# Moving the load of the last norm's scales and shifts ahead of the gathered rows in the sync engine's queue

## The chip, the cores and the metric

One NeuronCore of a Trainium2 chip runs one program. The metric is the device time of one execution in microseconds, lower being better. The kernel before was timed three times: median 1456.06 us, lowest 1455.17, highest 1457.25.

## The reference, cut to what matters

The program computes one layer of a streaming encoder on 320 tokens of width 1024 (256 of a prompt, 64 of a running stream): an input norm, a projection, three token mixers, an output projection with a norm, and then a mixture of 64 experts with a last norm. Only that last part is touched here:

```
s     = sigmoid(t @ w_router); the 8 best experts of each token, from the 4 best of 8 groups
gates = the chosen s, divided by their sum, times 2.5
hid   = silu(t @ exp_w1[e]) * (t @ exp_w3[e])
moe   = sum over the chosen e of gates[e] * (hid @ exp_w2[e])  +  the shared expert
y     = layer_norm(2**0.25 * t + moe) * ln2_g + ln2_b
```

The two vectors `ln2_g` and `ln2_b`, 1024 floats each, are the last norm's scales and shifts. All of it is float32.

## The kernel before, in words

**Experts.** The 64 experts are worked off as 32 pairs (`NP`). For pair n the tensor engine (PE) gathers the pair's tokens (`gather`, L1250), multiplies them by the up weights (`hidden`, L1283, matmuls on L1290), turns the result (`turn`, L1294, on L1298) and multiplies it by the down weights (`down`, L1301, on L1309). VectorE (DVE) makes the product of the two halves of the hidden rows (`hid_step`, L2560). The 128 result rows of a pair are scaled and, for pairs 0 to 29, written by GpSimd with an indirect DMA into a DRAM table `expert_rows` that has eight slots for each token (`scatter`, L2840). The last two pairs are not written: PE adds them on chip with one-hot matrices (`combine`, L1315, on L1320).

**Weights.** SyncE (SP) issues all weight loads from one queue. Each expert has 2 MB of up weights (`up_weights`, L642) and 1 MB of down weights (`down_weights`, L645), in a ring of three pairs. The up weights of pair n are issued when the hidden matmuls of pair n-3 are done, and its down weights when all of pair n-3 is done (L663 to L669). So the last two issues, the down weights of pair 31, come when pair 28 is done.

**Gathered rows.** Then SP waits until pair 29 is done and its rows have been written (L679, L680) and loads the table back in five pieces of 2 MB, `ROWS[0]` to `ROWS[4]`. Pieces 1 to 4 are `rows_in(0)` to `rows_in(3)` (L671 to L684): two pieces for each of the first two groups of 128 tokens. The fourth waits for pair 30, too, since its place holds that pair's weights. Piece 5 (L689) holds the last 64 tokens.

**The change's own line.** Between piece 4 and piece 5, SP loads `ln2_g` and `ln2_b` into the tile `LN2` (L685 to L687): two loads of 512 KB, each one row of 4 KB that is read for all 128 partitions. Before them stands a wait for the gather of pair 24 (`x_done`), since `LN2` lies where the rows of that and of earlier pairs were fetched to (`XR`, L282).

**The sums.** DVE folds piece 1 once before it makes the hidden rows of the last pair (L2610 to L2612), then adds piece 1 to the shared expert's rows, piece 2 after it (`sum_rows`, L327, with L331, L333 and L336), and tells PE with `added`, count 1 (L2636). Then it folds piece 3 and adds the shared rows (count 2, L2639), and folds piece 4 once (count 3, L2640). PE waits for count 1 ahead of L1388 (`add_kept`, L1328), for count 2 ahead of the first part of L1395 and for count 3 ahead of its second part, which ends the sums of token group 1. Piece 5 goes to PE without DVE (L1398 to L1402).

**The norm.** For each group of tokens in turn DVE waits for `tokens` (L2672), and, from group 1 on, takes the mean and the variance itself (L2680 to L2686). It scales by `LN2` and writes `y` (L2690, L2696). ScalarE (ACT) does these sums for group 0, makes the reciprocal roots and copies half of `LN2` for the last group (L1795 to L1810). DVE waits for `LN2` on L2670, ACT on L1804. SP writes `y` out, group by group (L704 to L709).

Of the kernel before, what the change touches and what calls it, by code (L numbers as in the profile page):

```python
# [17 lines left out]
D = 1024  # L18
# [60 lines left out]
FETCHED = (3, 4, 5, 6, 7, 8, 12, 18, 24)  # L79
# [7 lines left out]
def hybrid_layer(nc, io):  # L87

    ctx = ExitStack()
    with ctx:  # L90
        sems = {}

        def sem(name):
            if name not in sems:
                sems[name] = ctx.enter_context(nc.semaphore(name))
            return sems[name]
# [34 lines left out]
        def shaped(v, *shape):  # L131
            names = "abcd"[:len(shape)]
            if len(shape) <= 1:
                return v
            return v.rearrange(f"p ({' '.join(names)}) -> p {' '.join(names)}",
                               **{k: s for k, s in zip(names[1:], shape[1:])})
# [143 lines left out]
        SHID, LN2 = shaped(CON[:, C_RST:C_RST + 2 * NTOK], 2, NTOK), shaped(HT[:, 0:2 * D], 2, D)  # L280
# [28 lines left out]
        def unit_in(u, i):  # L309

            ring, _, n = unit_weights(u)
            if ring is WOS:
                return f"early_in_or_rows_in{i}", n
            return f"weights_in{i}", 16 * ((NT + RING - 1 - i) // RING + 3 + n)
# [65 lines left out]
        def _(sp):  # L380
# [290 lines left out]
            def rows_in(k):  # L671
                t = k // 2
                if k < 4:
                    rows = slots[t * 1024:t * 1024 + 1024, :].rearrange("(p k) d -> p k d", k=8)[:, k % 2 * 4:k % 2 * 4 + 4, :]
                else:
                    rows = slots[2048 + (k - 4) * 256:2304 + (k - 4) * 256, :].rearrange("(p k) d -> p k d", k=4)
                sp.dma_start(ROWS[k][0:128 if k < 4 else 64], rows).then_inc(sem(f"early_in_or_rows_in{k}"), 16)

            sp.wait_ge(sem("pair_done"), SENT)  # L679
            sp.wait_ge(sem("rows_out"), SENT + 2)  # L680
            for k in range(4):
                if k == 3:
                    sp.wait_ge(sem("pair_done"), SENT + 1)
                rows_in(k)  # L684
            sp.wait_ge(sem("x_done"), FETCHED[-1] + 1)  # L685
            for k in range(2):
                sp.dma_start(LN2[:, k, :], io['lnv'][4 + k:5 + k, :].to_broadcast([128, D])).then_inc(sem("ln_in"), 16)  # L687
            rows = slots[2048:SLOTS, :].rearrange("(p k) d -> p k d", k=4)
            sp.dma_start(ROWS[4], rows).then_inc(sem("x_first_or_halves_in"), 16)  # L689
            with sp.If(more > 0):  # L690
# [2009 lines left out]
        def _(pool):  # L2700
# [106 lines left out]
            def token_sums(q):  # L2807

                B11, B12, B21, B22 = (OTS[q][:, k * KH:k * KH + KH, h] for k in range(2) for h in range(2))
                T1, T2, _, T4 = MSUM[q]  # L2810
                ptt(T1, B12, B11, sub)
                pool.drain()
                ptt(T2, B22, T1, sub)
                pool.drain()
                ptt(T4, B21, T2, sub)
                pool.drain()
# [205 lines left out]
```

## Time and profile before

| what | us |
|---|---|
| median of three runs | 1456.06 |
| lowest and highest run | 1455.17, 1457.25 |
| the profiled execution's own time | 1456.23 |
| its span, from the first to the last instruction | 1454.4 |
| PE busy in the span | 1424.0 |
| DVE busy in the span | 723.6 |

The rows below all belong to the profiled execution, and their times count from the start of its span. It took 0.17 us more than the median, and 1.8 us of it lie outside the span. A busy PE is modelled from the starts of pipelined matmuls, so a share near 100% says that it was always fed and not that it ran at its peak. A DMA is issued by an engine's queue and lands when the last of the 16 DMA engines has written its share.

### The profile page before, as it was taken

What the parts mean: (1) busy time and instruction counts of PE and PEld (TensorE: products, weight loads), DVE (VectorE), ACT (ScalarE), POOL (GpSimd) and SP (SyncE); (2) the same over time, 40 slices, a digit from 0 to 9 for tenths busy, and PEclk for the clock granted to TensorE, in tenths of its full rate; (3) what the DMA queues carried; (4) which work ended last, traced back from release to release, by engine and by line L of the source; (5) the groups of instructions that cost most, each with busy time, mean ns of one, the idle gap of its engine ahead of it and who ended that gap; (6) DMA issues with size and microseconds to landing.
All of it is one profiled execution on the core that took longest, in us unless ns stands there. A gap on an engine that the chain in (4) does not pass through costs nothing.

```text
span 1454.4 us, 32377 instructions
## 1 busy us (share of the span) xinstructions
PE 1424.0 (98%) x13553; PEld 1032.2 (71%) x13553; DVE 723.6 (50%) x1360; ACT 411.4 (28%) x847; POOL 220.6 (15%) x183
## 2 busy tenths in 40 slices
PE   7999999999999999999999999999999999999997
PEld 6999677677776777777778985864476766757752
DVE  7442778887655677735457664523312112111217
ACT  2333444443422454434532211111111111111112
POOL 3784113130110000020013000011010000100000
PEclk9999999999999999999999999999999999999999
DMA  8896473754244544566567639699999999999986
GB/s 282 192 192 156 127 218 107 202 173 135 73 130 141 141 116 120 184 185 188 158 227 206 214 119 387 238 407 410 427 425 428 428 428 428 427 427 428 428 353 281
DMA packets 157761, 375.74 MB, mean 258 GB/s; under 512 B 102224, under 2 KB 110816, under 8 KB 139824
## 3 DMA queue, kind: packets, MB, share of 16 engines
q1 hardware_dynamic: 141792, 346.64, 67.5%
q0 software_dynamic: 7152, 16.85, 3.4%
q10 hardware_dynamic: 8672, 10.20, 2.0%
q8 instruction: 105, 1.72, 0.5%
q14 instruction: 40, 0.33, 0.1%
HBM read 329.24 MB, written 51.95 MB: 262 GB/s over the span
## 4 chain that ended last, share of the span: by engine, by line
PE 83%; DMA 7%; DVE 5%; DVEq 1%; ACT 1%; issue 1%; SPq 0%; ACTq 0%
PE PS L723 22%; PE PS L1290 13%; PE PS L740 7%; PE PS L1309 6%; PE PS L1136 6%; DMA region<-moe_w 5%; PE PS L1257 5%; PE PS L807 3%; PE PS L1178 2%; DVE region L1815 2%; DVE region L1822 2%; PE PS L1117 2%; PE PS L1262 1%; PE PS L1200 1%; PE PS L815 1%
## 5 line engine op out<-in xcount | busy, mean ns | idle before, releaser
L723 PE MATMUL PS<-h0T,region 128*128 128x320 f32 x1360 | 390.3, 438 | 1.8 <-issue 1.6
L1422 ACT ACTIVATE region<-PS 128x320 f32<-128x320 f32 (+5 forms) x351 | 145.8, 427 | 669.5 <-PE PS L723 227.5
L723 PEld LDWEIGHTS PS<-h0T,region 128*128 128x128 f32 x1360 | 251.6, 190 | 109.7 <-issue 13.1
L1290 PE MATMUL PS<-region 128*64 128x512 f32 x1024 | 228.2, 592 | 3.0 <-DMA region<-moe_w 3.0
L1290 PEld LDWEIGHTS PS<-region 128*64 128x64 f32 x1024 | 118.1, 137 | 104.6 <-issue 53.1
L1815 DVE TENSOR_TENSOR region<-region 128x512 f32<-128x512 f32 (+10 forms) x237 | 164.7, 714 | 41.0 <-DMA region<-expert_rows 7.8
L1422 ACT ACTIVATE region<-region 128x256 f32<-128x256 f32 (+10 forms) x229 | 99.5, 465 | 109.6 <-DVEq L2235 24.5
L1309 PE MATMUL PS<-region,history 128*64 128x512 f32 x512 | 119.2, 597 | 1.4 <-ACTq L1755 0.5
L1815 DVE TENSOR_TENSOR history<-region,PS 128x256 f32<-128x256 f32 x32 | 13.5, 421 | 202.0 <-ACTq L1750 201.9
L1422 ACT ACT_TABLE_LOAD x77 | 98.8, 1283 | 24.9 <-ACTq L1469 9.5
L1822 DVE SCALAR_TENSOR_TENSOR region<-region,feature_vectors 128x320 f32<-128x320 f32 (+1 forms) x103 | 76.8, 746 | 56.3 <-ACTq L1498 41.1
L1257 PEld LDWEIGHTS PS<-region,h 128*128 128x128 f32 x736 | 85.8, 192 | 16.1 <-issue 15.9
L1257 PE MATMUL PS<-region,h 128*128 128x128 f32 x736 | 92.0, 278 | 0.0
L1309 PEld LDWEIGHTS PS<-region,history 128*64 128x64 f32 x512 | 52.6, 137 | 42.8 <-issue 21.3
L2540 DVE COPY region<-PS 128x512 f32<-128x512 f32 x32 | 22.1, 692 | 122.0 <-PE PS L1273 96.8
L1136 PE MATMUL PS<-region 128*128 128x160 f32 x528 | 74.1, 299 | 0.3 <-ACTq L1695 0.3
L1136 PEld LDWEIGHTS PS<-region 128*128 128x128 f32 x528 | 72.5, 190 | 0.6 <-issue 0.5
L1422 ACT ACTIVATE region<-PS,region 128x512 f32<-128x512 f32 (+1 forms) x35 | 24.5, 699 | 146.6 <-PE PS L1309 146.3
L740 PE MATMUL PS<-region 128*128 128x160 f32 x448 | 65.4, 299 | 0.0
L740 PEld LDWEIGHTS PS<-region 128*128 128x128 f32 x448 | 62.4, 190 | 0.0
L1815 DVE TENSOR_TENSOR region<-region,PS 128x160 f32<-128x160 f32 (+3 forms) x95 | 43.2, 489 | 34.7 <-PE PS L740 14.7
L807 PEld LDWEIGHTS PS<-region 64*64 64x64 f32 x2720 | 49.8, 134 | 14.3 <-issue 12.0
(248 smaller groups left out, 1579.8 us busy)
## 6 DMA issues: line engine op xcount, KB each, us to landing
region<-moe_w SPq DMA_DIRECT2D x65, 2048.0 KB, 29.1
region<-moe_w SPq DMA_DIRECT2D x65, 1024.0 KB, 27.5
region<-w_in SPq DMA_DIRECT2D x115, 512.0 KB, 5.9
region<-wo SPq DMA_DIRECT2D x32, 512.0 KB, 4.4
expert_rows<-region SPq DMA_DIRECT2D x20, 512.0 KB, 7.0
region<-expert_rows SPq DMA_DIRECT2D x5, 2048.0 KB, 18.7
projected<-region ACTq DMA_DIRECT2D x59, 167.5 KB, 3.9
region<-projected SPq DMA_DIRECT2D x10, 768.0 KB, 6.6
```

What stands on the lines that cost most here:

```text
L723: last = mm(PS[:, 6 + i % 2, 0:NTOK], WR[:, i, k, :], H0T[:, k, :], start=(k == 0), stop=(k == KT - 1))
L740: last = mm(out, lhs(k), rhs(k), start=start and k == 0, stop=k == KH - 1, skip_group_check=True)
L807: last = mm(head(out(j), 1 - x if across and j > 3 else x), head(lhs(j), x), head(rhs(j), x), **kw)
L1117: last = mm(PS[:, b, 0:NTOK], WR[:, q, k, :], OT[:, 8 * q + k, :], start=(k == 0 and q < 3), stop=(k == KT - 1 and q != 2))
L1136: last = mm(out, lhs(k), rhs(k), start=start and k == 0, stop=k == KH - 1, skip_group_check=True)
L1178: last = mm(PS[:, 2 * t + h, :], MG[:, k, t * 128:t * 128 + 128], WOUT[:, k, h * 512:h * 512 + 512], start=(k == 0), stop=(k == KT - 1))
L1257: last = mm(bank(h, 4, 128)[:, k], H0[:, t, (4 * h + k) * 128:(4 * h + k) * 128 + 128], OH[:, p, t, :], start=(h == 0 and k == 0 and t == ...
L1290: last = mm(PS[tiles(i), 2, :], XE[:, k, tiles(i)], W13[r][i][:, k * 512:k * 512 + 512], start=(k == 0), stop=(k == KT - 1))
L1309: last = mm(PS[tiles(i), 5 + h, :], HIDT[:, f, tiles(i)], W2[r][i][:, f * D + h * 512:f * D + h * 512 + 512], start=(f == 0), stop=(f == 1))
L1422: return nc.scalar.activation(out, in_, f, **kw)
L1815: return dve.tensor_tensor(out, a, b, op)
L1822: return dve.scalar_tensor_tensor(out=out, in0=a, scalar=s, in1=b, op0=op0, op1=op1)
```

## The change

The wait for `x_done` and the two loads of `LN2` move, unaltered, from between piece 4 and piece 5 to a place behind the down weights of the last pair and ahead of the waits for pair 29 and its written rows.

```
+            sp.wait_ge(sem("x_done"), FETCHED[-1] + 1)
+            for k in range(2):
+                sp.dma_start(LN2[:, k, :], io['lnv'][4 + k:5 + k, :].to_broadcast([128, D])).then_inc(sem("ln_in"), 16)
             sp.wait_ge(sem("pair_done"), SENT)
             sp.wait_ge(sem("rows_out"), SENT + 2)
             for k in range(4):
                 if k == 3:
                     sp.wait_ge(sem("pair_done"), SENT + 1)
                 rows_in(k)
-            sp.wait_ge(sem("x_done"), FETCHED[-1] + 1)
-            for k in range(2):
-                sp.dma_start(LN2[:, k, :], io['lnv'][4 + k:5 + k, :].to_broadcast([128, D])).then_inc(sem("ln_in"), 16)
             rows = slots[2048:SLOTS, :].rearrange("(p k) d -> p k d", k=4)
             sp.dma_start(ROWS[4], rows).then_inc(sem("x_first_or_halves_in"), 16)
```

## Rows read from the trace of the kernel before

**Rows 1.** Page, part 4: the chain that ended last, whole span, by engine.
```profile
PE 83%; DMA 7%; DVE 5%; DVEq 1%; ACT 1%; issue 1%; SPq 0%; ACTq 0%
```

**Rows 2.** Chain of waits, 1421 us to the end: start, length, what.
```profile
1421.95 3.63 PE PS L1320 x8
1425.58 0.23 PE PS L1298 x2
...
1426.30 3.65 PE PS L1309 x16
...
1432.75 1.72 PE PS L1328 x4
...
1437.19 5.36 PE PS L1395 x12
...
1442.57 0.70 DVE region L2680
```

**Rows 3.** Timeline of DVE from 1410 us: start, length, instructions [idle before <-releaser].
```profile
1420.65 2.29 DVE L1815 TENSOR_TENSOR region<-region 128x2048 f32<-128x2048 f32 x1 [7.78 <-DMA region<-expert_rows]
1423.03 0.42 DVE L1815 TENSOR_TENSOR history<-region,PS 128x256 f32<-128x256 f32 x1
...
1426.18 2.29 DVE L331 TENSOR_TENSOR region<-region 128x2048 f32<-128x2048 f32 x1
...
1429.85 1.23 DVE L336 TENSOR_TENSOR region<-region 128x1024 f32<-128x1024 f32 x1
1431.19 7.30 DVE L1815 TENSOR_TENSOR region<-region 128x2048 f32<-128x2048 f32 x4
1439.31 1.28 DVE L1822 SCALAR_TENSOR_TENSOR region<-PS,region,h0T 128x1024 f32<-128x1024 f32 x1 [0.81 <-ACTq L1793]
```

**Rows 4.** Timeline of PE and its weight loads, 1437 us to 1447 us.
```profile
1438.58 0.19 PEld L1395 LDWEIGHTS PS<-region,constants 128*128 128x128 f32 x1 [0.31 <-DVEq L2590]
...
1442.37 1.02 PE L1326 MATMUL PS<-region,constants 128*128 128x512 f32 x2
...
1443.33 3.65 PE L1401 MATMUL PS<-region,constants 128*64 128x512 f32 x16
```

**Rows 5.** Timeline of SP's queue from 1360 us: its DMA issues.
```profile
1380.96 0.80 SPq L646 DMA_DIRECT2D region<-moe_w  x2
1409.79 5.66 SPq L677 DMA_DIRECT2D region<-expert_rows  x4
1415.49 0.95 SPq L687 DMA_DIRECT2D h0T<-lnv  x2
1416.48 0.43 SPq L689 DMA_DIRECT2D region<-expert_rows  x1
```

**Rows 6.** DMA issues singly (at 1381.3, 1409.8, 1410.2, 1411.7, 1415.1, 1416.0, 1416.5): us to landing.
```profile
region<-moe_w SPq DMA_DIRECT2D x1, 1024.0 KB, 34.5
region<-expert_rows SPq DMA_DIRECT2D x1, 2048.0 KB, 10.8
region<-expert_rows SPq DMA_DIRECT2D x1, 2048.0 KB, 15.3
region<-expert_rows SPq DMA_DIRECT2D x1, 2048.0 KB, 18.7
region<-expert_rows SPq DMA_DIRECT2D x1, 2048.0 KB, 20.2
h0T<-lnv SPq DMA_DIRECT2D x1, 512.0 KB, 21.9
region<-expert_rows SPq DMA_DIRECT2D x1, 2048.0 KB, 26.2
```

**Rows 7.** Stretches: busy us per engine, granted PE clock, DMA share, GB/s.
```profile
1408.00:1410.00 2.00, 2.00 (x18) 1.91 (x18) 0.00 (x0) 0.97 (x2) 0.00 (x0) 1.00 0.28 119
...
1440.00:1442.00 2.00, 2.00 (x6) 0.81 (x5) 1.83 (x3) 1.04 (x1) 0.00 (x0) 1.00 0.06 25
1450.00:1452.00 2.00, 0.00 (x0) 0.00 (x0) 0.90 (x2) 0.00 (x0) 0.00 (x0) 0.50 0.00 0
```

More of the change, by code:

```diff
@@ L677, in rows_in @@
                 sp.dma_start(ROWS[k][0:128 if k < 4 else 64], rows).then_inc(sem(f"early_in_or_rows_in{k}"), 16)
+            sp.wait_ge(sem("x_done"), FETCHED[-1] + 1)
+            for k in range(2):
+                sp.dma_start(LN2[:, k, :], io['lnv'][4 + k:5 + k, :].to_broadcast([128, D])).then_inc(sem("ln_in"), 16)
             sp.wait_ge(sem("pair_done"), SENT)
@@ L684, in _ @@
                 rows_in(k)
-            sp.wait_ge(sem("x_done"), FETCHED[-1] + 1)
-            for k in range(2):
-                sp.dma_start(LN2[:, k, :], io['lnv'][4 + k:5 + k, :].to_broadcast([128, D])).then_inc(sem("ln_in"), 16)
             rows = slots[2048:SLOTS, :].rearrange("(p k) d -> p k d", k=4)
```

## The prediction

> **What bounds the kernel now.** I read the page first: the chain that ended last is PE's work for 83% of the span [rows 1]. The change touches only the last 75 us, so all else is read there. The chain of waits shows what ends the run: PE without a gap through the combining of the last pairs (L1320), the last pair's turn and down matmuls (L1298, L1309), the sums over the gathered rows (L1328, L1395), and then DVE's norm of group 1 and group 2 [rows 2]. Next I asked how far PE is ahead of its suppliers. DVE's timeline shows that it is not ahead at all: DVE idles 7.78 us for piece 1, starts at 1420.65, and from there works without a break until 1431.19 + 7.30 = 1438.49, when piece 4 is folded [rows 3]. PE's weight load for the second part of L1395 stands at 1438.58 with DVE's fold as its releaser, not "issue" [rows 4]. So PE and DVE reach that point together, within a tenth of a microsecond, and DVE's part of it starts when piece 1 lands. Two chains of equal length end the kernel, and one of them hangs on a DMA.
>
> Then the DMA view, one issue at a time. SP issues the last down weights at 1381.3, pieces 1 to 4 from 1409.8, the scales and shifts at 1415.5 and 1416.0, and piece 5 at 1416.5 [rows 5]. Adding each issue's time to landing [rows 6] gives when the last share of each lands: down weights 1381.3 + 34.5 = 1415.8; piece 1 1409.8 + 10.8 = 1420.6; piece 2 1425.5; piece 3 1430.4; piece 4 1435.3; the shifts 1437.9; piece 5 1442.7. The steps are 4.8, 4.9, 4.9, 4.9, 2.6 and 4.8 us: 2 MB always take the same time and 1 MB half of it. Nothing waits for an issue in this row of landings, although piece 1 was issued 6 us before the weights had landed. Yet most DMA engines were idle then: from 1408 to 1410 the DMA share is 0.28, some 4.5 of 16 engines, and from 1440 to 1442, with piece 5 still under way, it is 0.06, one engine [rows 7]. I read this as **one DMA engine that is late**. It carries its share of everything in the order of issue, has not stopped between the last weights and piece 5, and sets each landing.
>
> **The change part by part.**
>
> *Issue on SP.* The wait for pair 24's gather and two issues (0.95 us) move to 1381.8. Pair 28 is done there, so the wait passes at once. SP issues nothing from 1381.8 to 1409.8 [rows 5], so 0.95 us there is covered; without that cover it would cost 0.95 us at piece 1. Piece 5 is issued 1 us earlier, which changes nothing while the late engine has a backlog.
>
> *The transfer, on 15 engines.* The 1 MB now lies behind the last weights, in the stretch where most engines run dry (0.28 busy). There it costs nothing. It also meets the indirect write of pair 29's rows, which gates piece 1's issue. An engine that writes rows beside weights now does so beside `LN2`. I take no delay: the issue at 1409.8 could slip by 8 us before the late engine, which would be busy until 1418.3, noticed.
>
> *The transfer, on the late engine.* Its weights end at 1415.8 as before. `LN2` follows, 2.5 us (the two ends in the trace are 1437.9 - 1435.3 = 2.6 and half of a piece, 2.4), to 1418.3. Pieces 1 to 4 then land 2.5 us later: 1423.1, 1428.0, 1432.9, 1437.8. Piece 5 lands at 1442.7 as before, since the same bytes stand ahead of it. Below, the cost is bounded by nothing (no late engine), above by 2.6.
>
> *DVE.* Its fold of piece 1 starts at 1423.1 in place of 1420.65, and all behind it follows by 2.5. The other pieces are there in time: L331 would start at 1428.7 with piece 2 landed at 1428.0, and piece 4's fold, the last 2.3 of the 7.30 us, at 1438.7 with the piece landed at 1437.8. So `added` is given at 1431.1 + 2.5 = 1433.6 (L336's end), at about 1436.2 + 2.5 = 1438.7 (the old end less the 2.29 of a fold of this shape), and at 1438.5 + 2.5 = 1441.0 [rows 3].
>
> *PE.* The last pair's hidden rows are ready at 1423.45 + 2.5 = 1425.95, where PE wants to turn them at 1425.58: it loses 0.4. L1328 would then start at 1433.1 and waits until 1433.6: 0.9 behind. L1395's first part would start at 1438.1 and waits until 1438.7: 1.5 behind. Its second part (old start 1438.58) waits until 1441.05: 2.5 behind [rows 2, 4]. What was cover turns into waiting four times over, but the lateness at the end is one 2.5 us and not a sum.
>
> *The end.* Group 1's norm starts at 1442.57 + 2.5. Group 0's doesn't hold it up: DVE did it between 1439.31 and 1442.57, in at most 3.3 us, and now has from 1441.0 to 1445.1. L1401 begins at 1443.33 + 2.5 = 1445.8 with piece 5 landed at 1442.7. Before, piece 5 landed just ahead of L1401 while PE was busy with L1326 until 1443.39 [rows 4], so an earlier piece 5 has nothing to give back.
>
> *Sum.* Issue 0, transfer +2.5, less the tenth by which PE was behind: span 1454.4 + 2.4 = 1456.8, execution 1456.23 + 2.4 = 1458.6. The execution was 0.17 above the median, so against the runs I expect 1456.06 + 2.4 = **1458.5 us**, 0.17% slower. A measurement of this kernel can tell about 0.2% from no change, 2.9 us, so this counts as no difference, though near its edge.
>
> **The rivals.**
>
> *It fits in the hole: no change.* If the late engine is an accident of the profiled execution, or runs level in most, the 1 MB is free. Piece 1 lands when its issue and 2 MB allow, and 1456.1 comes out (1455.3 to 1457.0 by the spread of the runs). For it: the share of 0.28. Against: equal steps in seven landings, which an engine with slack would not show. The Trainium skill would choose this rival: "DMA: Bandwidth & Descriptors", Rules for kernel authors, says to issue a DMA early and wait for it late, so that its cost overlaps; by that rule the time is 1456.1. The trace agrees that the issue is covered and disagrees on the transfer. The same page of the Trainium skill, Latency and other measured facts, says that two of the engines are usually slower than the rest and puts that, as a guess, down to the descriptor rings of GpSimd's DMAs. No view here tells engines apart; the trace agrees in so far as one is late, and by that rule it would be late in every execution. Chance 0.20.
>
> *PE's new waits cost it its clock: clearly slower.* The place is the wait ahead of L1395's second part, where PE would idle some 0.5 us after 0.4 to 0.6 three times before. Where PE stood idle from 1447 on, the granted clock is 0.50 (1.2 of 2.4 GHz) in the stretch from 1450 [rows 7]. Were that to happen at 1441, the 8 matmuls left of L1395 (two thirds of 5.36, 3.6 us) would take twice as long: 1458.5 + 3.6 = 1462.1. It decides from the point at which a wait is long enough for the clock to fall. Against: ACT's turn copy leaves PE idle for 0.5 us ahead of 1426.30 today and the clock stays at 1.00 later [rows 2, 7]. Chance 0.05.
>
> *Piece 5 and `LN2` were late: faster.* If the norm really waited for `LN2` (1437.9) or PE for piece 5, moving the loads would give time back. DVE first reads `LN2` at 1439.31, after a wait for ACT [rows 3], and PE is busy as piece 5 lands. At most the 0.1 us between PE's matmuls comes back: 1455.9. Chance 0.05, nearly all of it inside the spread of the runs.
>
> **How the numbers follow.** The forecast has 0.70, the rivals 0.20, 0.05 and 0.05. The range holds the forecast with its bounds and the spread of the runs (1457.2 to 1460.0) and most of the free case: 1455.5 to 1460.0. More than 0.2% slower means above 1459.0. The forecast lies 0.5 below that, and medians of runs that differ by 2 us pass it about a quarter of the time: 0.18, with 0.05 for the clock 0.23. Faster by 0.2% means below 1453.1, for which only an unknown part of the last rival is left: 0.03. The rest, 0.74, is within 0.2%.
>
> **What would show it.** Right: DVE's first fold starts near 1423.1 with some 10 us of idle time ahead of it, PE waits for DVE ahead of L1298, L1328 and both parts of L1395, the down weights still land near 1415.8 and piece 1 near 1423.1, piece 5 at 1442.7, and the last norm starts 2.5 us later. Wrong: piece 1 landing at 1420.6 or sooner (the free case), PE's clock below 1.00 before 1447 (the second rival), or the last weights landing later than 1416, which would mean that `LN2` does not queue behind them.

## The result, and the profile after

The changed kernel is slower by a little: 1459.37 us median of 16 runs (1457.63 to 1463.66) against 1457.24 of 16 runs of the kernel before (1455.17 to 1459.45). The ratio is 1.0019 with a 95% interval of 1.0011 to 1.0026, so 2.8 us (1.6 to 3.8); the medians differ by 2.1.

The profiled execution has a span of 1455.9 us and took 1457.63, the fastest of the 16. Its expert stage came to the last weights 0.8 us earlier than in the profile before (1380.15 against 1380.96 [rows 5]), so the two are compared from that issue on. These are SP's DMA issues in the changed kernel (start, length, what), to be held against [rows 5]:

```profile
1380.15 0.80 SPq L646 DMA_DIRECT2D region<-moe_w  x2
1381.00 7.19 SPq L681 DMA_DIRECT2D h0T<-lnv  x2
1408.98 5.66 SPq L677 DMA_DIRECT2D region<-expert_rows  x4
1414.68 0.44 SPq L689 DMA_DIRECT2D region<-expert_rows  x1
```

The two loads now stand right behind the last weights. Their issue takes 7.19 us in place of 0.95, but SP has nothing else to do until 1408.98, and the pieces go out 28.8 us behind the weights, as before. The next rows are the issues singly, with the us from issue to the last landing, for the second load of down weights (issued at 1380.5), the shifts (1382.8), piece 1 (1409.0), piece 4 (1414.3) and piece 5 (1414.7). They answer to [rows 6]:

```profile
region<-moe_w SPq DMA_DIRECT2D x1, 1024.0 KB, 34.5
...
h0T<-lnv SPq DMA_DIRECT2D x1, 512.0 KB, 34.7
...
region<-expert_rows SPq DMA_DIRECT2D x1, 2048.0 KB, 13.4
...
region<-expert_rows SPq DMA_DIRECT2D x1, 2048.0 KB, 22.6
...
region<-expert_rows SPq DMA_DIRECT2D x1, 2048.0 KB, 27.1
```

Added up: weights 1415.0, shifts 1417.5, piece 1 1422.4, piece 4 1436.9, piece 5 1441.8. The weights need 34.5 us as before. Then come 2.5 us of scales and shifts, and only then piece 1: 7.4 us behind the weights where it was 4.8. Piece 5 lands 26.8 us behind the weights, as before (1442.7 - 1415.8 = 26.9). The same bytes have changed places, and no gap has closed.

The stretches show where the hole was filled, and that one straggler is left (columns as in [rows 7]):

```profile
1408.00:1410.00 2.00, 2.00 (x30) 1.86 (x28) 0.00 (x0) 0.27 (x1) 0.00 (x0) 1.00 0.57 209
...
1440.00:1442.00 2.00, 1.70 (x4) 0.87 (x5) 1.19 (x2) 1.42 (x2) 0.00 (x0) 1.00 0.05 20
```

From 1408 to 1410 the DMA share went from 0.28 to 0.57: most engines take the early load in time that was idle. The share of 0.05 at 1440 is again about one engine of 16.

The trace also keeps 16 separate landings of each piece, one for each engine's share, though not the engine's number. These are the 16 of piece 1, in us from the issue of the last down weights, and they settle what the DMA shares only suggest:

| kernel | most of the 16 | the next | the last |
|---|---|---|---|
| before | 13 from 35.6 to 36.3 | 37.2, 37.2 | 39.67 |
| changed | 12 from 35.8 to 36.2 | 39.5, 39.6, 40.2 | 42.20 |

For twelve engines the early load is free, as in the rival that fits it into the hole. The last share alone sets when DVE may start: it was 2.4 us behind the next before, and it lands 2.5 us later now. Three more shares are late as well, but not as far. DVE's timeline follows piece 1:

```profile
1422.37 2.29 DVE L1815 TENSOR_TENSOR region<-region 128x2048 f32<-128x2048 f32 x1 [10.31 <-DMA region<-expert_rows]
1424.75 0.42 DVE L1815 TENSOR_TENSOR history<-region,PS 128x256 f32<-128x256 f32 x1
...
1427.90 2.29 DVE L331 TENSOR_TENSOR region<-region 128x2048 f32<-128x2048 f32 x1
...
1432.91 7.30 DVE L1815 TENSOR_TENSOR region<-region 128x2048 f32<-128x2048 f32 x4
1441.02 1.28 DVE L1822 SCALAR_TENSOR_TENSOR region<-PS,region,h0T 128x1024 f32<-128x1024 f32 x1 [0.81 <-issue]
```

The distances between its steps are those of [rows 3] to 0.02 us, up to the end of the 7.30. Its wait for the DMA is 10.31 us in place of 7.78: 2.53 more. PE's waits from 1405 to the end of the span (line, releaser, total us, times, longest) are four where there were none, beside the old one for ACT:

```profile
PE PS L1309 <- ACTq L1755: 0.5, 1, 0.5
PE PS L1298 <- DVEq L2563: 0.5, 1, 0.5
PE PS L1395 <- DVEq L2590: 0.4, 1, 0.4
PE PS L1395 <- DVEq L2639: 0.3, 1, 0.3
PE PS L1328 <- DVEq L341: 0.2, 1, 0.2
```

And the chain that ended last no longer runs through PE's combining. From 1408 to 1440 it is a DMA and DVE:

```profile
1408.98 13.37 DMA region<-expert_rows
...
1422.37 2.29 DVE region L1815
...
1437.92 2.29 DVE region L1815
...
1440.30 3.71 PE PS L1395 x8
...
1444.05 0.70 DVE region L2680
```

From the last down weights to group 1's norm it is 1444.05 - 1380.15 = 63.90 us, against 1442.57 - 1380.96 = 61.61 before [rows 2, 5]: 2.3 us longer.

### The profile page after: what moved, and what is told of

It reads as the page before. It is cut to its first block, busy times and chain, and to the rows that moved or that the text cites. A ratio compares the mean times of both kernels' runs of the same rounds, so it can differ in the third digit from the quotient of the medians.

```text
span 1455.9 us, 32377 instructions
## 1 busy us (share of the span) xinstructions
PE 1425.0 (98%) x13553; PEld 1031.5 (71%) x13553; DVE 724.4 (50%) x1360; ACT 411.8 (28%) x847; POOL 221.2 (15%) x183
## 4 chain that ended last, share of the span: by engine, by line
PE 80%; DMA 10%; DVE 5%; ACT 1%; issue 1%; DVEq 1%; SPq 1%; ACTq 0%; POOLq 0%
PE PS L723 22%; PE PS L1290 12%; PE PS L740 7%; PE PS L1309 6%; PE PS L1136 5%; DMA region<-moe_w 5%; PE PS L1257 5%; PE PS L807 3%; DVE region L1815 2%; PE PS L1178 2%; PE PS L1117 2%; PE PS L1262 1%; PE PS L1200 1%; PE PS L815 1%; DVE region L1822 1%
```

## The experiments

Each profile is read by one number beside its time: from the issue of the last down weights to DVE's first fold of piece 1. It is 1420.65 - 1380.96 = 39.7 us before and 1422.37 - 1380.15 = 42.2 after. A second number is the distance from that issue to group 1's norm, 61.61 us before and 63.90 after. All rows below come from timelines (start, length, instruction) unless the text says otherwise.

The runs with half the load, with half as much again, without a load and with the load between pieces 3 and 4 share 29 runs of the kernel before (median 1458.53). The runs with shorter rows and with split loads share 17 (1457.41), and the three around the later issue 29 (1456.36). The us behind a ratio are that ratio's share of this median; the difference of the two medians can lie up to 1.1 us away from it. The edits are shown against the changed kernel (`...` stands for code that is not printed), but for the load between pieces 3 and 4 and the first run with a later issue, which are shown against the kernel before. Where the number of loads changes, the count that is waited for at `ln_in` changes with it; only the run without a load shows this.

**Half the load.**

```
-            for k in range(2):
+            for k in range(1):
                 sp.dma_start(LN2[:, k, :], ...)
...
                 rows_in(k)
+            sp.dma_start(LN2[:, 1, :], ...)
             rows = slots[2048:SLOTS, :]
```

> The scales alone go behind the last weights; the shifts stay between piece 4 and piece 5. Theory (one late DMA engine takes every byte in the order of issue and has no gap from the last weights to piece 5, so each 512 KB ahead of piece 1 delays pieces 1 to 4 by 1.2 us): 1.2 us over the kernel before, piece 1 landing 6.0 to 6.1 us behind the last down weights in the profile (4.8 before, 7.4 with both). Rival (it is the place in SP's queue, or the wait that moved, and not the bytes): as with both, 2.1 to 2.5 us over.

Measured: 1458.99 us, ratio 1.0002 (0.9992 to 1.0013): 0.3 us, and -1.2 to 1.9.

```profile
1382.76 0.80 SPq L646 DMA_DIRECT2D region<-moe_w  x2
...
1423.99 2.29 DVE L1816 TENSOR_TENSOR region<-region 128x2048 f32<-128x2048 f32 x1 [9.31 <-DMA region<-expert_rows]
...
1445.65 1.29 DVE L2681 BATCH_NORM_STATS2 region<-PS 128x6 f32<-128x512 f32 x2
```

The fold starts after 41.2 us, 1.5 later than before and 1.0 sooner than with both loads. That speaks for the bytes, though the first 512 KB cost 1.5 us there and the second 1.0, not 1.2 each (piece 1 lands 6.4 us behind the weights, where 6.0 to 6.1 were expected). Group 1's norm starts after 62.89 us, 1.3 later than before: near the theory's 1.2, and well below the rival's 2.1. The measured time agrees and just shuts out 2.1; alone it could not show 1.2 against nothing.

**Half as much again.**

```
             for k in range(2):
                 sp.dma_start(LN2[:, k, :], ...)
+            for v in (HT[:, 2 * D:2 * D + 512], CON[:, C_RST:C_RST + 512]):
+                sp.dma_start(v, io['lnv'][4:5, 0:512].to_broadcast([128, 512])).then_inc(sem("ln_in"), 16)
```

> Both loads go behind the last weights, and behind them two further loads of 256 KB that nobody reads (the first 512 scales for all partitions, into idle places). Theory: 1.5 MB ahead of piece 1 cost 3.7 us over the kernel before, and piece 1 lands 8.5 us behind the last down weights. Piece 5 lands 1.2 us later than in either kernel, which PE does not notice. Rival (not the bytes): as with both, 2.1 to 2.5 us over.

Measured: 1464.27 us, ratio 1.0044 (1.0032 to 1.0057): 6.4 us (4.7 to 8.3).

```profile
1382.31 0.81 SPq L646 DMA_DIRECT2D region<-moe_w  x2
1383.16 6.83 SPq L681 DMA_DIRECT2D h0T<-lnv  x2
1390.03 3.78 SPq L683 DMA_DIRECT2D h0T<-lnv  x1
1393.86 2.10 SPq L683 DMA_DIRECT2D constants<-lnv  x1
...
1427.76 2.29 DVE L1817 TENSOR_TENSOR region<-region 128x2048 f32<-128x2048 f32 x1 [13.54 <-DMA region<-expert_rows]
```

The fold starts after 45.45 us, 5.8 later than before, and the time follows it. So a delay of piece 1 still reaches the end well past 2.5 us. The size was wrong: the added 512 KB cost 3.2 us at piece 1 and not 1.2, and as much at piece 5, for which PE still does not wait. That bytes alone set the price does not hold for these two loads. The landings show the same pattern as in the changed kernel: the last share of piece 1 lands after 45.4 us, while the first ten still land between 36.2 and 36.5.

**The same bytes in shorter rows**, to see whether the 2 KB rows of those two loads were the reason.

```
             for k in range(2):
-                sp.dma_start(LN2[:, k, :], io['lnv'][4 + k:5 + k, :].to_broadcast([128, D])) ...
+                for f in (0, 512):
+                    sp.dma_start(LN2[:, k, f:f + 512], io['lnv'][4 + k:5 + k, f:f + 512].to_broadcast([128, 512])) ...
```

> As the changed kernel, but each load is cut into two of 512 columns, so the same 1 MB comes in rows of 2 KB in place of 4 KB. Theory (bytes count): as the changed kernel, piece 1 7.4 us behind the last down weights, 2.1 to 2.5 us lost. Rival (the short rows cost more on the late engine, as the two loads added in the run with 1.5 MB suggest, whose 512 KB cost 3.5 us where 1.2 were expected): piece 1 lands 10 us or more behind, and 5 us or more are lost.

Measured: 1459.49 us, ratio 1.0015 (1.0007 to 1.0024): 2.2 us (1.0 to 3.5).

```profile
1379.69 0.80 SPq L646 DMA_DIRECT2D region<-moe_w  x2
1380.53 13.00 SPq L682 DMA_DIRECT2D h0T<-lnv  x4
...
1421.96 2.29 DVE L1816 TENSOR_TENSOR region<-region 128x2048 f32<-128x2048 f32 x1 [10.37 <-DMA region<-expert_rows]
```

After 42.3 us, as in the changed kernel. Neither the row length nor the number of loads is the price; the bytes are, here. Why the 512 KB to other places cost 3.2 us (the expectation has 3.5) stays open.

**No load at all.** The last norm's scales and shifts are left out, so `y` is computed with whatever lies in their place.

```
-            sp.wait_ge(sem("x_done"), FETCHED[-1] + 1)
-            for k in range(2):
-                sp.dma_start(LN2[:, k, :], ...)
...
-            dve.wait_ge(sem("ln_in"), 96)
+            dve.wait_ge(sem("ln_in"), 64)
```

> The scales and shifts are not loaded at all: the last norm uses what stands in their place, so y is left out of account. Theory: pieces 1 to 4 as in the kernel before, piece 5 lands 2.5 us sooner, and nothing waited for it: the time of the kernel before, within 0.5 us. Rival (the norm or PE waited for the shifts or for piece 5 in the kernel before): 0.5 to 2.5 us faster.

Measured: 1458.75 us, ratio 1.0001 (0.9993 to 1.0010): 0.1 us (-1.0 to 1.5).

```profile
1385.61 0.80 SPq L646 DMA_DIRECT2D region<-moe_w  x2
...
1425.39 2.29 DVE L1812 TENSOR_TENSOR region<-region 128x2048 f32<-128x2048 f32 x1 [7.87 <-DMA region<-expert_rows]
...
1447.22 1.30 DVE L2677 BATCH_NORM_STATS2 region<-PS 128x6 f32<-128x512 f32 x2 [0.29 <-PE PS L1392]
```

After 39.8 us, as before, and the norm after 61.61, as before. In the old place the load cost nothing that these runs can tell, so no other place for it can gain: at most 1.0 us by the interval.

**Between piece 3 and piece 4.**

```
                 if k == 3:
+                    for j in range(2):
+                        sp.dma_start(LN2[:, j, :], ...)
                     sp.wait_ge(sem("pair_done"), SENT + 1)
                 rows_in(k)
-            sp.wait_ge(sem("x_done"), FETCHED[-1] + 1)
-            for k in range(2):
-                sp.dma_start(LN2[:, k, :], ...)
```

> Both loads stand between piece 3 and piece 4. Theory: pieces 1 to 3 land as before, piece 4 2.5 us later, at 1437.8 where DVE is free for it at 1436.2 (old scale): 1.6 us over the kernel before, and DVE waits 1.6 us for a DMA ahead of its last fold. Rival (only the start of DVE's chain, at piece 1, counts): no change. Rival (any place ahead of piece 5 costs the whole transfer): 2.5 us over.

Measured: 1460.37 us, ratio 1.0016 (1.0007 to 1.0024): 2.3 us (1.0 to 3.5).

```profile
1382.98 0.80 SPq L646 DMA_DIRECT2D region<-moe_w  x2
...
1422.68 2.29 DVE L1814 TENSOR_TENSOR region<-region 128x2048 f32<-128x2048 f32 x1 [7.79 <-DMA region<-expert_rows]
...
1433.22 4.89 DVE L1814 TENSOR_TENSOR region<-region 128x2048 f32<-128x2048 f32 x3
1439.75 2.29 DVE L1814 TENSOR_TENSOR region<-region 128x2048 f32<-128x2048 f32 x1 [1.64 <-DMA region<-expert_rows]
...
1445.87 1.29 DVE L2679 BATCH_NORM_STATS2 region<-PS 128x6 f32<-128x512 f32 x2
```

DVE starts piece 1 after 39.7 us, as before, and loses 1.64 us ahead of its last fold, where 1.6 was expected. So it is not only the start of the chain that counts. The time shuts out "no change", but cannot tell 1.6 from 2.5; the rows can: group 1's norm starts after 62.89 us, 1.3 later than before, where the changed kernel has 2.3.

**A later issue of the pieces**, in both kernels: if one engine that is still busy with the weights sets piece 1's landing, the issue can be late without harm.

```
-            sp.wait_ge(sem("pair_done"), SENT)
+            sp.wait_ge(sem("pair_done"), SENT + 1)
             sp.wait_ge(sem("rows_out"), SENT + 2)
```

> The kernel before, but SP issues no piece until pair 30 is done, so pieces 1 to 3 go out about 5.3 us later, at 1415.1 on the old scale; nothing else changes. Theory (one late engine is busy with the weights until 1415.8 and sets piece 1's landing): that engine does not notice; the others, idle until the issue, need 4.9 us for 2 MB and 1 to 2 us to begin, and land piece 1 at 1421 to 1422 in place of the late one's 1420.6, so 0.4 to 1.4 us are lost. Rival (piece 1 lands some 11 us behind its issue, as all engines get to it): piece 1 and DVE's chain 5.3 us later, and 5 us lost.

> The changed kernel with the same later issue. Theory: the late engine is busy until 1418.3 with the weights and the early load, the others land piece 1 by 1421 to 1422 and it lands at 1423.1 as in the changed kernel: no difference from the changed kernel run beside it (2.1 to 2.5 us over the kernel before), within 0.7 us. Rival: 5 us over the changed kernel.

> The changed kernel itself, beside the two others: 2.1 to 2.5 us over the kernel before, piece 1 in use 41.9 us behind the issue of the last down weights (39.3 before).

Measured: with the kernel before 1458.32 us, ratio 1.0014 (1.0005 to 1.0023), 2.0 us; with the changed kernel 1458.25 us, 1.0016 (1.0007 to 1.0025), 2.3 us; the changed kernel alone 1457.47 us, 1.0015 (1.0007 to 1.0024), 2.2 us (1.1 by the medians). In that last run the fold starts after 1421.80 - 1379.58 = 42.2 us, as in the first profile of the changed kernel (the expectation counts from the second load of the weights, 0.37 us later). First the kernel before with the later issue, then the changed kernel with it:

```profile
1379.99 0.80 SPq L646 DMA_DIRECT2D region<-moe_w  x2
1414.16 1.99 SPq L677 DMA_DIRECT2D region<-expert_rows  x4
...
1421.57 2.29 DVE L1815 TENSOR_TENSOR region<-region 128x2048 f32<-128x2048 f32 x1 [9.67 <-DMA region<-expert_rows]
```

```profile
1380.05 0.80 SPq L646 DMA_DIRECT2D region<-moe_w  x2
1380.90 7.20 SPq L681 DMA_DIRECT2D h0T<-lnv  x2
1414.22 1.85 SPq L677 DMA_DIRECT2D region<-expert_rows  x4
...
1422.28 2.29 DVE L1815 TENSOR_TENSOR region<-region 128x2048 f32<-128x2048 f32 x1 [10.31 <-DMA region<-expert_rows]
```

The issue comes 34.2 us behind the weights in both, where it was 28.8. In the kernel before the fold starts after 41.6 us: 1.9 late for an issue that is 5.3 late. All 16 shares of piece 1 now land between 41.0 and 41.6, so the late one has caught up and the issue sets the piece. From that issue to the fold it is 7.4 us (1414.16 to 1421.57), a little more than I had allowed. In the changed kernel the fold starts after 42.2 us, as without the later issue: 5.3 us of delay vanish altogether, since the last share lands after 42.2 as before and the other fifteen have come by 41.8. So with the issue as early as it is in both kernels, it is a backlog behind the weights that sets piece 1, and not the issue.

**Loads cut so that not every engine carries them**, to name the late engine.

```
-                sp.dma_start(LN2[:, k, :], ... .to_broadcast([128, D])) ...
+                for a, b in ((0, 120), (120, 128)):
+                    sp.dma_start(LN2[a:b, k, :], ... .to_broadcast([b - a, D])) ...
```

> As the changed kernel, but each of the two loads is cut into one for partitions 0 to 119 and one for partitions 120 to 127. Theory (one late engine): if the larger part is shared among 15 engines and the late one is the engine left out, piece 1 lands 4.8 to 5.3 us behind the last down weights as in the kernel before, and the time is that of the kernel before within 0.7 us; if the late one is among the 15, piece 1 lands 7.4 us behind or a little more and 2.1 to 2.8 us are lost. Rival (all engines are about equally late, or the place in the queue costs): 2.1 to 2.5 us lost, with no third outcome. The Trainium skill, in DMA: Bandwidth & Descriptors, on why a DMA increments its semaphore by 16, says that a load runs on as many engines as divide its slowest dimension, up to 16: 15 for 120 partitions and 8 for 8.

The other run replaces the two lines added by `for a in range(0, 128, 8)` with loads of `LN2[a:a + 8, k, :]`.

> As the changed kernel, but each of the two loads is cut into 16 loads of 8 partitions. Theory: if a load of 8 partitions runs on 8 engines, these carry twice their share, 4.9 us. If the late engine is one of them, piece 1 lands 9.7 us behind the last down weights and 4.5 to 5 us are lost; if not, piece 1 lands at most 7.4 behind, set by the next latest engines, and 0 to 2.5 us are lost. Rival (every engine gets its sixteenth whatever the cut): as in the changed kernel, 7.4 us behind and 2.1 to 2.5 us lost. If SP cannot issue 32 loads before pair 29 is written, its timeline shows the pieces issued later, and that part of the loss is not the engines'.

Measured: 1463.95 us, ratio 1.0047 (1.0034 to 1.0060), 6.8 us with the cut at 120; 1467.45 us, 1.0076 (1.0061 to 1.0092), 11.1 us with loads of 8 partitions. Neither theory had a place for that much. The 32 small loads also held SP past the time at which the pieces could go out:

```profile
1382.38 0.80 SPq L646 DMA_DIRECT2D region<-moe_w  x2
1383.22 31.66 SPq L682 DMA_DIRECT2D h0T<-lnv  x32
1414.99 2.82 SPq L677 DMA_DIRECT2D region<-expert_rows  x4
...
1430.91 2.29 DVE L1816 TENSOR_TENSOR region<-region 128x2048 f32<-128x2048 f32 x1 [16.62 <-DMA region<-expert_rows]
```

With the cut at 120 SP had issued its loads in time, but the pieces still went out 30.7 us behind the weights in place of 28.8, since the rows of pair 29 were written later:

```profile
1380.06 0.80 SPq L646 DMA_DIRECT2D region<-moe_w  x2
...
1410.80 3.75 SPq L677 DMA_DIRECT2D region<-expert_rows  x4
```

The rate changed, too. One stretch of 12 us, first of the changed kernel, then of the one with the cut (columns as in [rows 7]):

```profile
1412.00:1424.00 12.00, 12.00 (x51) 4.28 (x48) 1.69 (x2) 1.76 (x3) 0.00 (x0) 1.00 1.01 431
```

```profile
1412.00:1424.00 12.00, 12.00 (x51) 4.19 (x48) 0.00 (x0) 1.76 (x3) 0.00 (x0) 1.00 0.98 341
```

The engines are as busy (0.98) and move a fifth less, 341 GB/s for 431, and the weights ahead of the loads landed late, too (37.1 us behind their issue in place of 34.5, in both runs). Even the first share of piece 1 came after 39.25 us with the cut at 120, where the changed kernel has 35.8. The number of engines is the one expected: beside one mark at each issue the trace has 46 and 256 landings of these loads, which is 15 for a load of 120 partitions and 8 for one of 8. But the cut slowed everything around it, so these two runs do not tell which engine is late. That stays open, and so does why one is.

## Why the prediction was right or wrong

*What bounds.* Right. PE and DVE reached the second part of L1395 together, and 2.5 us more on DVE's side made DVE and the DMA ahead of it the chain that ended last.

*One engine that is late.* Borne out as far as a backlog behind the last weights: the fold moves with the megabytes ahead of piece 1 (39.7 us with none, 41.2 with 0.5 MB, 42.2 with 1) and ignores 5.3 us of a later issue in the changed kernel. That one share is last by itself is shown by the landings (39.67 before and 42.20 after, 2.4 and 2.0 us behind the next), and with them by the shares of 0.05 and 0.06 at 1440. It is no accident of one execution: the profiles without a load and with the load between pieces 3 and 4 have 39.75 and 39.68, and the repeat of the changed kernel 42.20. That it is the same engine each time is likely by the equal steps, but not shown, and the runs with split loads did not name it.

*Issue on SP.* The cost of nothing is right, the size is not: 7.19 us in place of 0.95, all of it under the 28 us in which SP waits.

*The transfer.* 2.5 us of forecast delay, 2.53 measured as DVE's added wait. The weights did not move (34.5 us), piece 5 kept its place, and the indirect write of pair 29 did not hold up the pieces. The slack of 8 us at the issue of piece 1 was too large: it looked at the late engine alone, while the others need 7.4 us from issue to use, so about 6 us are left of it (1423.1 less 7.4 less 1409.8), of which 5.3 were tried.

*DVE and PE.* DVE's steps kept their distances. PE's four new waits came at the places named, as 0.5, 0.2, 0.3 and 0.4 us. By the forecast lateness (0.4, 0.9, 1.5 and 2.5) they would be 0.4, 0.5, 0.6 and 1.0; the second rival has 0.5 for the last, which does not fit that. Three of the four waits came out shorter than that, and why is not shown. The lateness behind them is as forecast: the second part of L1395 starts 1440.30 - 1380.15 = 60.15 us behind the weights, against 1438.58 - 1380.96 = 57.62 [rows 4, 5], 2.5 later. PE's clock stayed at 1.00 through 1442, which is the second rival's end.

*The rival that fits the load into the hole.* Its place is there (the share went to 0.57), but a hole on most engines is none on the one that ends last. The Trainium skill's rule for kernel authors in "DMA: Bandwidth & Descriptors", issue early and wait late, names the fixed setup cost as what overlaps. The trace agrees on that much: all 7.19 us of issue are covered. The prediction took the rule for the whole transfer when it worked out 1456.1 by it; on the engine that lands last the transfer did not overlap, and 2.8 us were lost (2.2 in the repeat).

*The sum.* 2.4 us of forecast loss stand against 2.8 (1.6 to 3.8) by the ratio, 2.1 by the medians and 2.3 in the profile; 1458.5 us stands against 1459.37. Of that 0.9, more than all is the kernel before, whose median over 16 runs is 1457.24 and not the 1456.06 of the first three.

*The step that failed* is the last of the sum: "A measurement of this kernel can tell about 0.2% from no change, 2.9 us, so this counts as no difference, though near its edge." With 16 runs a side the interval of the ratio reaches 0.08% to either side, 1.1 us. The forecast of 0.17% was a forecast of slower, and it was put in words and in the chances (0.74 for no difference) as one of no change. What the runs showed in its place is a slowdown clear of no change, 0.11% to 0.26%. The mechanism and its price were right; the 2.9 us that a measurement was said to need stand in the prediction without a reason (the three runs known then spread over 2.1 us), and they are more than twice what 16 runs a side needed.

## What to carry to other kernels

Where one share of a DMA queue's loads is behind, as here, there is no free place ahead of the load that somebody waits for: an early issue moves its bytes in front of that load, and here 1 MB cost 2.5 us although most DMA engines had idle time for it. Look for the engine that ends last (equal steps between landings, a small DMA share beside a load still under way) and not at the mean share, and put what is needed late behind what is needed soon. Before a load is moved, leave it out once: if that gains nothing, no place for it can.

## What the runs showed of the hardware that I had not expected

- Of the 16 shares of each of the pieces 1 to 4 one landed 2.4 to 2.6 us behind the next in the kernel before, while thirteen landed within 1.1 us of one another. With the pieces issued 5.3 us later the 16 shares of piece 1 landed within 0.6 us.
- Issuing two loads of 512 KB took SP 7.19 us behind a backlog of weights, and 0.95 in the old place [rows 5]; why is not shown. 32 loads of 32 KB took 31.66 us.
- Loads of 120 and 8 partitions slowed the transfers around them: 341 GB/s at a DMA share of 0.98, where whole loads had 431 at 1.01.
- Two loads of 256 KB to other tiles held piece 1 up by 3.2 us, where the first 512 KB of whole loads took 1.5, and rows of the same length in `LN2` cost nothing beyond that.
